# Each column part of the last four down tiles loaded by three transfers of 112, 8 and 8 partitions instead of one of 128

## The chip, the cores and the metric

The kernel runs on one core of one Trainium2 chip. The metric is the device time of one execution in microseconds (us): lower is better. The times given are medians of several executions; the profile shows one execution, with its own time beside it.

## The reference, cut to what matters

One layer of a trunk for 128 context tokens and 128 latent tokens (256 in all), model width 1024, float32. After the token mixers comes a mixture of 64 experts, and its weights are nearly all that the kernel loads: three arrays of 64 x 1024 x 256 float32, 64 MB each.

```python
def expert_block(args):
    tb, gb = args
    a = jax.nn.silu(jnp.einsum('td,edf->tef', tb, w_gate)) * jnp.einsum('td,edf->tef', tb, w_up)
    return jnp.einsum('tef,efd->td', a * gb[..., None], w_down)
...
x = x + g2 * moe_ffn(hn, ...)
```

Every expert's gate and up projection (1024 to 256) and its down projection (256 back to 1024) are applied to the tokens routed to it, the results are summed over the experts per token, and a gated residual gives the outputs `y_prompt` and `y_sample`.

## The kernel before

**Tiles and loops.** The weights of an expert are three tiles of 1 MB (gate, up, down), each 128 partitions x 8 KB. Four experts make a unit; 16 units are computed in sequence, the experts ordered by how many tokens they got. The tiles rotate through a ring of twelve places and five more (`spare`, `gb`, `xn`, a place over `yhi`, `rows_tile`); `PLACE` says which tile goes where. The last unit is a "quad" unit: four experts side by side, 32 token slots each.

**Who loads.** SyncE (SP) issues all expert tiles, in one order, in its own program: `released(g)` waits until TensorE has finished with the tile whose place is to be filled, then `load_tile` (L577) issues one 1 MB transfer on all 128 partitions. Its semaphore `tile_loaded[place]` rises by 16 when it has landed. TensorE waits for that semaphore in `weights_ready` before the matmuls that use the tile.

**The end.** The last four down tiles are treated apart. `lay_out_by_columns` has arranged `w_down` so that a range of output columns is contiguous in each partition. `FINAL` names three column parts in the order in which they are loaded and computed: columns 512 to 1024, 256 to 512 and 0 to 256. For each part `load_columns` (L649) issues one transfer per tile, twelve in all: 128 partitions x 4 KB (512 KB) for the first part, and 128 partitions x 2 KB (256 KB) for the second and the third. The first two parts count on `last_columns[0]` and `last_columns[1]` (four transfers each, so 64), the third on each tile's own `tile_loaded`. SP starts them when the down matmuls of the quad step before have released the places (`y_filled`, by the matmuls of L1365).

**What uses them.** `down_final` on TensorE (matmuls at L1343) waits for part 0, multiplies, waits for part 1, multiplies, then adds parts 0 and 1 into the token sums (`combine_final`: L1323 with the upper halves `yhi`, L1327 with the rests `ylo`), and then waits for part 2. ScalarE makes `yhi` (L1763) and VectorE `ylo` (L2365) of each of the first two parts; VectorE then multiplies the sums with the gate (`scale`, L2437), GpSimd adds the residual (L835), and SP and ScalarE store the outputs (L531). Part 2 goes by a shorter way: VectorE gates it in place (L2383), TensorE spreads it to tokens (L1318), VectorE adds it (L2388).

**Other names in the diff.** `weights_ready(..., again=True)` is for later rounds, which run only if an expert got more tokens than its slots hold; the trace ends after the first round.

Of the kernel before, what the change touches and what calls it, by code (L numbers as in the profile page):

```python
# [44 lines left out]
PAIR, QUAD = 2, 4  # L45
# [3 lines left out]
NSLOT = 4  # L49
NTILE = 3 * NSLOT  # L50
# [11 lines left out]


UNITS = NE // NSLOT
QUAD_UNITS = {12 // 2 * it + 2 + j for it in range(TURNS) for j in range(2)} | {UNITS - 2, UNITS - 1}
FIRST_STEP = [sum(1 if v in QUAD_UNITS else 2 for v in range(u)) for u in range(UNITS)]

# [5 lines left out]
def place_tiles():  # L73

    place, replaces, free = list(FILL), [None] * len(FILL), []
    taken = 0
    while len(place) < UNITS * NTILE:
        if len(place) == ROWS_FREE:
            place.append(OVER_ROWS)
            replaces.append(None)  # L80
        kept = OVER_Y if len(place) < (UNITS - 1) * NTILE else OVER_GB
        while place[taken] == OVER_Y or (kept == OVER_GB and place[taken] in (OVER_GB, OVER_XN)):
            taken += 1
        place.append(place[taken])
        replaces.append(taken)
        taken += 1
    nth = [place[:g + 1].count(p) for g, p in enumerate(place)]
    return place, replaces, nth


PLACE, REPLACES, NTH = place_tiles()


def build(nc, t, o, overflow_at=CAP):

    ctx = ExitStack()
    with ctx:
# [6 lines left out]
        def sem(name):  # L104
            return ctx.enter_context(nc.semaphore(name))
# [264 lines left out]
        tile_loaded = [sem(f"tile_loaded{i}") for i in range(NTILE + 5)]  # L370
        last_columns = [sem(f"last_columns{i}") for i in range(2)]
# [106 lines left out]
        def tile(i):  # L478
            if i >= NTILE:
                return (spare[:, :], gb[:, :, :].rearrange("p s d -> p (s d)"), xn[:, 0:EW], over_yhl[:, :], rows_tile[:, :])[i - NTILE]  # L480
            return ring[:, i * EW:(i + 1) * EW]
# [3 lines left out]
        down_dram = t["w_down"]  # L485

        def down_columns(weights, f, cols_):

            v = weights.rearrange("p (q j n) -> p j q n", j=JF, q=D // FE)[:, f, cols_.start // FE:cols_.stop // FE, :]
            return v[:, 0, :] if v.shape[1] == 1 else v  # L490

        def tile_of(kind, par, part, j):
            return 4 * part + j if kind == QUAD else 6 * par + 2 * part + j

        def unit_of(kind, par, unit):
            return unit + par if kind == QUAD else unit
# [11 lines left out]
        def final_out(i):  # L508

            return bank[FINAL_BANK[i]][:, FINAL[i].start % 512:FINAL[i].start % 512 + FINAL[i].stop - FINAL[i].start]  # L510
# [22 lines left out]
        def weights_of(kind, par, part, j, unit, again):  # L533

            i = tile_of(kind, par, part, j)
            return tile(i if again else PLACE[unit_of(kind, par, unit) * NTILE + i])

        def weights_ready(pe, kind, par, part, j, unit, again):

            i = tile_of(kind, par, part, j)  # L540
            if again:
                pe.wait_ge(tile_loaded[i], unit * 16 + (PLACE.count(i) * 16 + 16))
            else:
                g = unit_of(kind, par, unit) * NTILE + i
                pe.wait_ge(tile_loaded[PLACE[g]], NTH[g] * 16)
# [6 lines left out]
        def _(sp):  # L552
# [21 lines left out]
            def load_tile(g, e):  # L574
                unit, i = divmod(g, NTILE)
                part = i // 4 if unit in QUAD_UNITS else i % 6 // 2
                sp.dma_start(tile(PLACE[g]), (gate_dram, up_dram, down_dram)[part][e]).then_inc(tile_loaded[PLACE[g]], 16)  # L577
# [50 lines left out]
            def after(step, part, more=0):  # L628

                if part == 0:  # L630
                    sp.wait_ge(gate_used, step + 1)
                elif part == 1:
                    sp.wait_ge(e_filled, step + 1)
                else:
                    sp.wait_ge(y_filled, step * 2 + 2 + more)

            def released(g):

                unit, i = divmod(g, NTILE)
                if unit in QUAD_UNITS:  # L640
                    after(FIRST_STEP[unit], i // 4)
                else:
                    after(FIRST_STEP[unit] + i // 6, i % 6 // 2)

            def load_columns(g, e, i):

                w = FINAL[i]
                v = slice(JF * w.start, JF * w.stop)
                ins = sp.dma_start(tile(PLACE[g])[:, v], down_dram[e][:, v])  # L649
                ins.then_inc(last_columns[i] if i < 2 else tile_loaded[PLACE[g]], 16)  # L650

            def refill(unit, experts, first=0, end=NTILE):

                for i in range(first, end):
                    g = unit * NTILE + i
                    if REPLACES[g] is None:
                        sp.wait_ge(sorted_filled, 1)
                        sp.wait_ge(cnt_ready, 1)
                    else:
                        released(REPLACES[g])  # L660
                    load_tile(g, experts[i % 4 if unit in QUAD_UNITS else 2 * (i // 6) + i % 2])

            def experts_of(unit):
                return [expert_at(NSLOT * unit + j) for j in range(NSLOT)]

            refill(1, range(NSLOT, 2 * NSLOT), first=len(FILL) - NTILE)
            sp.wait_ge(order_ready, 1)
            for unit in range(2, UNITS - 1):
                refill(unit, experts_of(unit))
            experts = experts_of(UNITS - 1)  # L670
            refill(UNITS - 1, experts, end=8)
            released(REPLACES[UNITS * NTILE - 1])
            for i in range(N_FINAL):
                for j in range(NSLOT):
                    load_columns(UNITS * NTILE - NSLOT + j, experts[j], i)
# [169 lines left out]
        def _(pe):  # L845
# [222 lines left out]
            for q in range(2):  # L1068
                ins = nc.tensor.transpose(ps[0:ROWS, q * P:q * P + P], gi[:, q, :], ident[:, :])
# [11 lines left out]
            ins = nc.tensor.transpose(ps[:, 4 * ROWS:4 * ROWS + NH], n0r[:, :], ident[0:NH, 0:NH])  # L1081
# [231 lines left out]
            def combine_final(i):  # L1313

                if i == LAST:
                    for s, y in ((1, act_e), (0, sil)):
                        pe.wait_ge(last_gated, 2 - s)
                        mm(last_sum(s), ptone[:, 1, s * P:s * P + P].bitcast(F32), y[:, :],  # L1318
                           start=True, stop=True).then_inc(all_done, 1)
                    return  # L1320
                pe.wait_ge(y_hi, (STEPS - 1) * 2 + (i + 1))
                for s in (1, 0):
                    mm(final_acc(s, i), ptone[:, 1, s * P:s * P + P], final_y(yhi, i), start=False, stop=False,  # L1323
                       skip_group_check=True)
                pe.wait_ge(y_lo, (STEPS - 1) * 2 + (i + 1))
                for s in (1, 0):
                    mm(final_acc(s, i), ptone[:, 1, s * P:s * P + P], final_y(ylo, i), start=False, stop=False,  # L1327
                       skip_group_check=True).then_inc(all_done, 1)

            def down_final(unit):  # L1330

                w = P // QUAD
                pe.wait_ge(a_copied, STEPS)
                pe.wait_ge(g2_kept, 2 * NST)
                for i, cols_ in enumerate(FINAL):
                    if i < 2:
                        pe.wait_ge(last_columns[i], 16 * NSLOT)
                    else:
                        for j in range(QUAD):
                            weights_ready(pe, QUAD, 1, 2, j, unit, False)  # L1340
                    for f in range(JF):
                        for j in range(QUAD):
                            ins = mm(final_out(i)[j * w:(j + 1) * w, :], actT[:, f, j * w:(j + 1) * w],  # L1343
                                     down_columns(weights_of(QUAD, 1, 2, j, unit, False), f, cols_),
                                     start=(f == 0), stop=(f == JF - 1))
                    ins.then_inc(y_filled, 1)
                    if i == 1:
                        combine_final(0)
                        combine_final(1)
                combine_final(2)  # L1350
# [43 lines left out]
            def two_steps(kind, e, n, group, unit, following, gates=gate_s, before=True, starts=False, shared=None, ends=False,  # L1394
# [40 lines left out]
                if ends:  # L1435
                    down_final(unit)
                else:
                    down(kind, 1, n + 1, unit, group, last, again)
# [1064 lines left out]
```

## Time and profile before

| what | value |
|---|---|
| median of 3 runs | 643.16 us (641.85 to 643.47) |
| the profiled execution, its time | 640.87 us |
| its span, first to last instruction | 639.6 us |
| TensorE matmul, busy | 579.2 us (91%) |
| TensorE weight load, busy | 404.3 us (63%) |
| VectorE, busy | 211.8 us (33%) |
| ScalarE, busy | 167.7 us (26%) |
| read from HBM | 250.06 MB, 394 GB/s over the span |

The page of a profile gives the busy time of each engine, the span cut in 40 slices, and the chain of work that ended last. The trace behind it can be asked for a stretch alone: its instructions in order of time, the chain of waits, the share of the DMA engines that was busy, and for a DMA the time from its issue to its landing. "SPq" is an issue of a DMA by SyncE's queue, "ACTq" one by ScalarE's.

### The profile page before, as it was taken

The page shows a single profiled execution, that of the slowest core. Times are in us where ns is not written, and L with a number is a line of the kernel's source. Part 1 is how long each engine was busy: PE and PEld are TensorE (multiplying, and loading weights), DVE is VectorE, ACT ScalarE, POOL GpSimd, SP SyncE. Part 2 cuts the span into 40 slices and gives each one's busy share as a digit, 9 for nine tenths or more (in the row PEclk, how much of TensorE's full clock was granted, in tenths as well). Part 3 has the DMA queues.
Part 4 walks back from the last instruction along what each step waited for, and adds up shares of the span by engine and source line. Part 5 has one row for each costly group of instructions (what it writes and reads, how often), then busy time and mean ns, then how long its engine had stood idle before and what let it go on. Part 6 is the DMA issues. An engine that isn't in the chain of part 4 may idle for free.

```text
span 639.6 us, 11143 instructions
## 1 busy us (share of the span) xinstructions
PE 579.2 (91%) x4568; PEld 404.3 (63%) x4568; DVE 211.8 (33%) x479; ACT 167.7 (26%) x308; POOL 32.8 (5%) x78
## 2 busy tenths in 40 slices
PE   0899999999999999989999999596999999997775
PEld 0488777788867676657575766364567666664343
DVE  1287867787832222011222121020121212121104
ACT  3164727672622121112121212010212121212110
POOL 1340210011100000000000000000000000000002
PEclk9989999999999999999999999798999999999889
DMA  8999699989999999999999999999999999999994
GB/s 341 386 344 388 216 363 381 409 327 397 419 378 379 404 421 419 422 420 420 421 420 421 420 421 419 421 421 421 421 420 420 421 420 421 420 421 419 422 412 159
DMA packets 49126, 252.55 MB, mean 395 GB/s; under 512 B 5912, under 2 KB 9632, under 8 KB 24752
## 3 DMA queue, kind: packets, MB, share of 16 engines
q1 hardware_dynamic: 46272, 245.85, 94.7%
q0 software_dynamic: 1840, 4.21, 2.0%
q10 hardware_dynamic: 960, 1.74, 0.7%
q8 instruction: 37, 0.61, 0.4%
q14 instruction: 17, 0.14, 0.1%
HBM read 250.06 MB, written 1.72 MB: 394 GB/s over the span
## 4 chain that ended last, share of the span: by engine, by line
PE 56%; DMA 20%; SPq 16%; ACT 4%; DVE 2%; issue 2%; POOL 0%; POOLq 0%; DVEq 0%; ACTq 0%
PE bank L1291 17%; SPq L577 14%; PE bank L1365 9%; DMA ring<-in_w_up 8%; DMA ring<-in_w_down 7%; PE bank L1262 5%; PE bank L1308 5%; PE bank L861 3%; DMA ring<-in_w_mod 2%; PE bank L903 2%; PE bank L911 2%; PE bank L907 2%; DMA ccol<-in_c 2%; SPq L649 1%; DMA ring<-in_w_in 1%
## 5 line engine op out<-in xcount | busy, mean ns | idle before, releaser
L1291 PE MATMUL bank<-ring,xe 128*64 128x256 f32 (+1 forms) x1520 | 176.4, 395 | 10.5 <-DMA ring<-in_w_up 9.3
L1291 PEld LDWEIGHTS bank<-ring,xe 128*64 128x64 f32 (+1 forms) x1520 | 110.9, 131 | 49.3 <-issue 23.0
L1365 PE MATMUL bank<-ring,actT 128*64 128x512 f32 (+1 forms) x384 | 83.9, 597 | 3.8 <-DMA ring<-in_w_down 2.2
L2339 DVE TENSOR_TENSOR act_e<-bank,sil 128x256 f32<-128x256 f32 x26 | 11.0, 425 | 192.1 <-ACT sil L1754 192.1
L2353 DVE SCALAR_TENSOR_TENSOR ylo<-bank,gslot,yhi 128x512 fp32r<-128x512 f32 x50 | 37.5, 751 | 78.1 <-ACT yhi L1767 78.1
L1767 ACT ACTIVATE yhi<-bank,gslot 128x512 fp32r<-128x512 f32 x50 | 34.4, 688 | 110.7 <-PE bank L1365 110.7
L1754 ACT ACTIVATE sil<-bank 128x256 f32<-128x256 f32 x26 | 10.0, 385 | 195.1 <-PE bank L1291 195.1
L1262 PE MATMUL bank<-pone,hhi 128*128 128x256 f32 x200 | 50.0, 288 | 0.0
L1262 PE MATMUL bank<-pone,hlo 128*128 128x256 f32 x200 | 48.9, 282 | 0.0
L1365 PEld LDWEIGHTS bank<-ring,actT 128*64 128x64 f32 (+1 forms) x384 | 25.0, 127 | 32.5 <-issue 32.3
L1291 PE MATMUL bank<-rows_tile,xe 128*64 128x256 f32 (+1 forms) x128 | 32.9, 416 | 12.5 <-DMA ring<-in_w_up 6.3
L1749 ACT ACTIVATE xe<-bank 128x512 f32<-128x512 f32 x50 | 29.9, 598 | 48.2 <-PE bank L1262 48.2
L1308 PE MATMUL bank<-yhi,ptone 128*128 128x512 f32 x100 | 42.2, 422 | 0.0
L1308 PE MATMUL bank<-ylo,ptone 128*128 128x512 f32 x100 | 39.5, 395 | 0.0
L1262 PEld LDWEIGHTS bank<-pone,hhi 128*128 128x128 f32 x200 | 38.2, 191 | 0.5
L1262 PEld LDWEIGHTS bank<-pone,hlo 128*128 128x128 f32 x200 | 38.1, 191 | 0.6
L1291 PE MATMUL bank<-xn,xe 128*64 128x256 f32 (+1 forms) x128 | 31.8, 406 | 3.3 <-DMA ring<-in_w_up 3.3
L1291 PEld LDWEIGHTS bank<-rows_tile,xe 128*64 128x64 f32 (+1 forms) x128 | 17.3, 137 | 25.1 <-issue 19.1
L1291 PE MATMUL bank<-spare,xe 128*64 128x256 f32 (+1 forms) x128 | 31.8, 406 | 0.0
L1291 PE MATMUL bank<-gb,xe 128*64 128x256 f32 (+1 forms) x128 | 31.8, 406 | 0.0
L835 POOL TENSOR_TENSOR xn<-xn,xt 128x512 f32<-128x512 f32 (+1 forms) x3 | 3.4, 1165 | 462.9 <-DVE xn L2437 462.9
L1308 PEld LDWEIGHTS bank<-yhi,ptone 128*128 128x128 f32 x100 | 18.7, 187 | 13.1 <-issue 9.8
(388 smaller groups left out, 849.0 us busy)
## 6 DMA issues: line engine op xcount, KB each, us to landing
ring<-in_w_gate SPq DMA_DIRECT2D x49, 1024.0 KB, 25.3
ring<-in_w_down SPq DMA_DIRECT2D x48, 1024.0 KB, 26.3
ring<-in_w_up SPq DMA_DIRECT2D x46, 1024.0 KB, 26.6
ring<-in_w_mod SPq DMA_DIRECT2D x12, 2048.0 KB, 13.6
ring<-in_w_in SPq DMA_DIRECT2D x5, 2048.0 KB, 15.4
gb<-in_w_up SPq DMA_DIRECT2D x5, 1024.0 KB, 25.3
spare<-in_w_gate SPq DMA_DIRECT2D x4, 1024.0 KB, 26.9
ring<-in_w_out SPq DMA_DIRECT2D x2, 2048.0 KB, 18.7
```

The source lines that it names most:

```text
L577: sp.dma_start(tile(PLACE[g]), (gate_dram, up_dram, down_dram)[part][e]).then_inc(tile_loaded[PLACE[g]], 16)
L861: ins = mm(ps[r:r + P // CT, 0:MW], csil[:, CT * a + k, :], w[:, k, MW * c:MW * c + MW], start=(a == 0 and k == 0), stop=(a == 1 and k == ...
L903: mm(ps[s][:, 0:w], xhi[:, k, s * P:s * P + P], proj_upper(c)[:, k, :], start=(k == 0), stop=False)
L907: mm(ps[s][:, 0:w], xlo[:, k, s * P:s * P + P], proj_upper(c)[:, k, :], start=False, stop=False)
L911: ins = mm(ps[s][:, 0:w], xhi[:, k, s * P:s * P + P], proj_rest(c)[:, k, :], start=False, stop=(k == KD - 1))
L1262: ins = mm(ps[:, k * 256:k * 256 + 256], h[:, s, 2 * q + k, :], pone[:, s, :, :].rearrange("p a b -> p (a b)"), start=(i == 0), stop=(i == 3))
L1291: ins = mm(bank[6][j * w:(j + 1) * w, part * FE:(part + 1) * FE], xe[:, k, slots], weights[:, k, :], start=(k == 0), stop=(k == KD - 1))
L1308: ins = mm(acc[s][n][:, :], ptone[:, par, s * P:s * P + P], y[:, n, :], start=(first and y is yhi), stop=False, skip_group_check=True)
L1365: ins = mm(bank[4 + h][j * w:(j + 1) * w, :], actT[:, f, j * w:(j + 1) * w], down_columns(weights_of(kind, par, 2, j, unit, again), f, sli ...
L1749: A(xe[:, 2 * q:2 * q + 2, :], bank[(7, 4, 5, 7)[q]][:, :].rearrange("p (a b) -> p a b", a=2), ACT.Copy).then_inc(x_copied, 1)
L1767: A(yhi[:, n, :], bank[4 + n][:, :], ACT.Copy, scale=gslot[:, par:par + 1]).then_inc(y_hi, 1)
L2353: V.scalar_tensor_tensor(out=ylo[:, n, :], in0=bank[4 + n][:, :], scalar=gslot[:, par:par + 1], in1=yhi[:, n, :].bitcast(F32), op0=ALU.mul ...
```

## The change

A tuple of three partition ranges is added, and each column part of each of the last four down tiles is issued once per range: 36 transfers instead of 12, of the same bytes. The counts that TensorE waits for grow with the number of transfers. Nothing else changes.

```diff
+LAST_ROWS = (slice(0, 112), slice(112, 120), slice(120, 128))
...
@@ weights_ready (later rounds only)
             if again:
-                pe.wait_ge(tile_loaded[i], unit * 16 + (PLACE.count(i) * 16 + 16))
+                more = (len(LAST_ROWS) - 1) * (i in PLACE[UNITS * NTILE - NSLOT:])
+                pe.wait_ge(tile_loaded[i], unit * 16 + ((PLACE.count(i) + more) * 16 + 16))
...
@@ load_columns
                 w = FINAL[i]
                 v = slice(JF * w.start, JF * w.stop)
-                ins = sp.dma_start(tile(PLACE[g])[:, v], down_dram[e][:, v])
-                ins.then_inc(last_columns[i] if i < 2 else tile_loaded[PLACE[g]], 16)
+                for rows_ in LAST_ROWS:
+                    ins = sp.dma_start(tile(PLACE[g])[rows_, v], down_dram[e][rows_, v])
+                    ins.then_inc(last_columns[i] if i < 2 else tile_loaded[PLACE[g]], 16)
...
@@ down_final
                     if i < 2:
-                        pe.wait_ge(last_columns[i], 16 * NSLOT)
+                        pe.wait_ge(last_columns[i], 16 * NSLOT * len(LAST_ROWS))
                     else:
                         for j in range(QUAD):
-                            weights_ready(pe, QUAD, 1, 2, j, unit, False)
+                            at = PLACE[UNITS * NTILE - NSLOT + j]
+                            pe.wait_ge(tile_loaded[at], (PLACE.count(at) - 1 + len(LAST_ROWS)) * 16)
```

## Rows read from the trace of the kernel before

**Rows 1.** The page, throughput of the DMA engines in 40 slices of the span.
```profile
GB/s 341 386 344 388 216 363 381 409 327 397 419 378 379 404 421 419 422 420 420 421 420 421 420 421 419 421 421 421 421 420 420 421 420 421 420 421 419 422 412 159
```

**Rows 2.** Chain of waits, 560 to 640 us: start, duration, what.
```profile
600.48 3.67 PE bank L1365 x32
...
613.15 15.50 DMA ring<-in_w_down
...
628.70 1.11 PE bank L1343 x16
...
630.34 0.38 DVE ylo L2365
...
630.77 0.70 DVE xn L2437
...
631.54 0.94 POOL xn L835
```

**Rows 3.** Busy time of each engine by stretch, and the DMA engines' share.
```profile
622.00:624.00 2.00, 2.00 (x37) 1.24 (x30) 0.00 (x0) 0.03 (x1) 0.00 (x0) 1.00 1.07 404
...
625.00:626.00 1.00, 1.00 (x7) 0.78 (x6) 0.42 (x1) 0.00 (x0) 0.00 (x0) 1.00 0.65 240
...
628.00:629.00 1.00, 0.47 (x12) 0.22 (x12) 0.00 (x0) 0.69 (x1) 0.00 (x0) 1.00 0.50 191
629.00:630.00 1.00, 1.00 (x17) 0.49 (x10) 0.75 (x1) 0.17 (x1) 0.00 (x0) 1.00 0.20 78
```

**Rows 4.** Packets from 628.7 to 631.3 us.
```profile
DMA packets 83, 0.14 MB, mean 55 GB/s; under 512 B 13, under 2 KB 13, under 8 KB 83
```

**Rows 5.** The page, queue that loads instructions: packets, MB, share of 16 engines.
```profile
q8 instruction: 37, 0.61, 0.4%
```

**Rows 6.** L649 from 615.2 us: the ninth transfer, issue, time to landing.
```profile
L649 SPq DMA_DIRECT2D spare<-in_w_down x1: 1921/1921/1921, 615.2 to 615.2; - x1
...
DMA to landing us min/median/max: 14.1/14.1/14.1
```

**Rows 7.** L649 from 618.8 us: the twelfth transfer, issue, time to landing.
```profile
L649 SPq DMA_DIRECT2D ring<-in_w_down x1: 2879/2879/2879, 618.8 to 618.8; - x1
...
DMA to landing us min/median/max: 12.4/12.4/12.4
```

**Rows 8.** Timeline, 627 to 632 us: start, duration, engine, line, operation.
```profile
627.13 0.60 PE L1343 MATMUL bank<-ring,actT 128*32 128x512 f32 x3
...
627.56 0.60 PE L1343 MATMUL bank<-ring,actT 128*32 128x512 f32 x3
628.23 0.69 ACT L1763 ACTIVATE yhi<-bank,gslot 128x512 fp32r<-128x512 f32 x1 [3.88 <-PE bank L1343]
...
629.02 0.75 DVE L2365 SCALAR_TENSOR_TENSOR ylo<-bank,gslot,yhi 128x512 fp32r<-128x512 f32 x1 [1.05 <-ACT yhi L1763]
...
631.37 0.38 PE L1343 MATMUL bank<-spare,actT 128*32 128x256 f32 x1
```

**Rows 9.** Chain of waits, the first five issues of L649.
```profile
604.31 0.33 SPq L649
...
604.82 0.52 SPq L649
...
606.63 1.99 SPq L649
```

**Rows 10.** Timeline of the start: two transfers of 8 partitions, three of 2 MB.
```profile
1.29 0.66 ACTq L1485 DMA_DIRECT2D bnr<-in_norm_w  x1
...
1.98 0.28 ACTq L1486 DMA_DIRECT2D bnr<-in_norm_w  x1
...
2.32 5.91 SPq L566 DMA_DIRECT2D ring<-in_w_mod  x3
```

**Rows 11.** The page, issues of full down tiles: count, KB each, median us to landing.
```profile
ring<-in_w_down SPq DMA_DIRECT2D x48, 1024.0 KB, 26.3
```

**Rows 12.** DMA issues from 560 us: an output store, median us to landing.
```profile
out_y_sample<-xn SPq DMA_DIRECT2D x1, 256.0 KB, 2.0
```

## Prediction

> **What bounds the kernel now.** I read the page's throughput slices first. From the fifteenth slice on they stand at 419 to 422 GB/s nearly without a break until the last two [rows 1]: the kernel is a stream of weights, and its end follows from when the last bytes land. So the question is the last 35 us. The chain of waits there says it plainly: the down matmuls of L1365 release the places at about 604.2, SP issues the twelve column transfers of L649, the eighth of them (part 1 of the last tile), issued at 613.15, takes 15.50 us and lands at 628.65, and TensorE starts part 1 at 628.70. Then come ScalarE's `yhi` (in between), VectorE's `ylo`, VectorE's `scale`, and GpSimd's residual at 631.54, which leads to the last stores [rows 2]. The third view is the stretches: the DMA engines are all busy until 624 (share 1.07, which is full), but only 0.65 from 625, 0.50 from 628 and 0.20 from 629 [rows 3]. The bytes are not short of bandwidth there; about half of the 16 engines have finished by 625 or 626, and the other half is still working. After part 1 has landed only some 70 packets of 2 KB remain (0.14 MB; the other 13 of the 83 are under 512 B), out of 512 that part 2 has [rows 4]. So the late engines set part 1 and part 2, and the early ones idle for up to 5 us.
>
> Why half of them is late can be estimated. The queue that loads instructions took 0.4% of 16 engines' span, in 37 packets [rows 5]: 0.004 x 16 x 639.6 = 41 us of one engine. If it falls on eight engines, it makes each of them 5.1 us late, about what the stretches show. That is an estimate; no row names an engine.
>
> **Part by part: the balance of rows.** A part's transfer has 128 rows, and one row is one packet [rows 4]; over 16 engines that is eight rows each. With 112 rows it is seven each. The two transfers of 8 rows can use at most eight engines each. If both go to the same eight, those carry 9 rows per tile and part and the others 7. If these others are the late ones, they lose one row in eight. The price of a row: the ninth transfer lands at 615.24 + 14.1 = 629.3 [rows 6] and the twelfth at 618.84 + 12.4 = 631.2 [rows 7], so three transfers of 2 KB rows take 1.9 us on the last engine, 0.64 each, 0.08 per row, and 0.16 for a 4 KB row. Until the end of part 1 that is four rows of 4 KB and four of 2 KB, 0.64 + 0.32 = 0.96 us earlier; until the end of part 2 it is 1.28 us. The early engines finish later by as much, at 626 or 627 instead of 625 or 626, and still in time.
>
> **What is late next.** Part 1 would land at 628.65 - 0.96 = 627.69. But TensorE is still in part 0: its last matmuls start at 627.56, 0.43 after those before them, so part 1 can start at about 628.0 [rows 8]. It gains 0.7, not 0.96. Behind it, ScalarE has `yhi` of part 0 until 628.92 and VectorE `ylo` of part 0 until 629.77 [rows 8]; VectorE can start `ylo` of part 1 at about 629.8 instead of 630.34 [rows 2], 0.54 earlier. `scale` then starts at about 630.3 instead of 630.77, and GpSimd follows. The gain that reaches the end is **0.5 us**. Part 2 would land at 631.2 - 1.3 = 629.9, and TensorE comes to it at 630.9 instead of 631.37 [rows 8]: no wait there. The bounds are 0 (another order of the same engines) and 0.96 (all of part 1's gain).
>
> **Part by part: the issues.** SP issues 36 transfers instead of 12. Four pitches before, from 604.31 to 606.63, are 0.58 us each, with durations of 0.33 and 0.52 and a gap of about 0.18 between two [rows 9]. For a transfer of 8 partitions the trace has two, on ScalarE's queue: 0.66 and 0.28 us [rows 10]. So a new pitch lies between 0.28 + 0.18 = 0.46 and 0.66 + 0.18 = 0.84; I take 0.58, since that is the same line and queue in the same state. The last issue then begins at 604.31 + 35 x 0.58 = 624.6, and lands at 626.6 at the earliest, with the 2.0 us of a store of 256 KB [rows 12] as latency. It is needed at 631.3. So the 24 added issues cost nothing, hidden behind the stream; without that cover they would cost 24 x 0.58 = 14 us. Behind them on SP stand only the stores, the first of which waits for GpSimd's work at 631.54 [rows 2]. The second term is whether SP is held. Before, the fifth issue took 1.99 us instead of 0.33 [rows 9], with some ten transfers in flight (a full tile lands 26.3 us after its issue [rows 11], and 1.05 MB at 421 GB/s [rows 1] are 2.5 us). At the start of the kernel SP was held with far fewer but larger ones: three of 2 MB took 5.91 us [rows 10]. So it is room for rows that runs out, not for transfers, and the rows stay the same. A few more entries for completion are added (two per tile and part on eight engines); I price them at nothing, and at 0.5 us at most. TensorE's waits have other counts and the same place.
>
> The 8-row transfers move 32 and 16 KB. The Trainium skill ("DMA: Bandwidth & Descriptors", Rules for kernel authors) says of such sizes that under 64 KB one pays mostly overhead, and to coalesce; its fixed cost of about 2 us, paid 24 times in a row, would make 48 us. That no run of this case pays it in series is told by ten transfers in flight at a time [rows 11].
>
> **Rivals.** *The rows go to the wrong eight.* If the 8-row transfers fall on the late engines, part 1 lands 0.96 later, 629.6, and the whole chain behind it moves: **+0.95 us**, 644.1. Nothing in the rows names the engines, so only the form speaks: a fixed choice of eight either hits the late set or misses it. The same page (Why a DMA increments its semaphore by 16 and not by 1) says that a transfer uses the largest number of engines up to 16 that divides its partitions, the lowest-numbered ones; by that 112 gives 16 engines and 8 gives the first eight, but which half fetches instructions it doesn't say.
>
> *Nothing changes.* The 8-row transfers alternate over all engines, or another wait stands at once behind part 1: **0**, 643.2. The same page's rule for two transfers to disjoint partitions (don't bother, they share the same engines) would give this. Against it: eight rows can't be on 16 engines.
>
> *SP becomes the bound, the case that ends slower.* The place is the last issues of part 2. It decides from a pitch of (631.3 - 2.0 - 604.31) / 35 = 0.71 us on. At 0.84 the last issue begins at 633.7 and lands at 635.7: **+4.4 us**. If instead SP is held by the number of transfers, it has issued ten by 620, when the last full tile is through, and the other 26 need 15 us: the last lands at 637.2, **+5.9**. For it: 0.66 in one row. Against: 0.28 in the other, and the pitch of 0.58 with four times the rows and more.
>
> **How the numbers follow.** The profiled execution has a span of 639.6 and a time of 640.87, 1.3 around the span; the median of the runs is 2.3 above that. I put the difference on the median: 643.16 - 0.5 = **642.7 us**. Chances: the forecast 0.47, the wrong eight 0.18, nothing changes 0.22, SP the bound 0.10, and 0.03 for a gain that I don't see. The range takes in the first three: from the lowest run less the upper bound of the gain, 641.85 - 0.96 = 640.9, to the highest run plus the loss, 643.47 + 0.95 = 644.4. Left out is SP as the bound, and half of the unseen gain. About 0.3% (1.9 us) is what a measurement of this kernel can tell from no change, and the first three cases all lie within it: 0.86. Slower by more is SP's case and a little for two losses at once, 0.11; faster 0.03.
>
> **What the profile after would show.** If the forecast holds: 36 issues of L649, done by about 625; the DMA share from 628 on below 0.50 and higher from 625; TensorE's idle time before part 1, now 628.70 - 628.16 = 0.54 us, near 0; `ylo` of part 1 directly behind that of part 0. If the wrong eight are loaded: that idle time grows to about 1.5 us, the DMA share stays high after 629. If SP is the bound: the last issue of L649 begins after 629, and TensorE waits before part 2. Wrong would be the prediction if the 24 issues are held (2 us each), or if the late engines are not a fixed set.

## The result, and the profile after

The changed kernel takes 650.47 us (median of four runs, 649.19 to 651.68) beside 642.5 us for the kernel before (640.64 to 646.54). The ratio is **1.012, with a 95% interval of 1.0076 to 1.0165**: slower, and outside the range that was forecast (642.7 us, 640.9 to 644.4). Two disturbed runs of it, at 744 and 2044 us, are left out. The profiled execution has a span of 648.5 us and a time of 649.75, against a span of 639.6 and 640.87 before. So 8.9 us have to be found. In the file after the change L649 is now L652, L1343 is L1347, L1291 is L1294 and L1211 is L1214.

The page's throughput slices are read first, as before [rows 1]. This is the page of the kernel after, from its start to its end:

```profile
GB/s 339 385 329 384 225 359 389 410 333 397 419 327 423 406 417 420 418 421 422 421 419 421 420 421 419 420 420 421 421 419 422 419 423 421 420 419 421 408 242 133
```

Before the last three slices only the twelfth and the thirteenth differ by more than 15 GB/s, and their sum hardly does (750 against 757). The second last slice has 242 GB/s instead of 412. A low value could mean that the DMA engines had run out of work. The stretches tell that they had not. First one row of the kernel before, then the kernel after; the last three columns are TensorE's granted clock, the DMA engines' busy share, and GB/s:

```profile
616.00:620.00 4.00, 3.00 (x14) 2.28 (x13) 0.00 (x0) 2.39 (x4) 0.00 (x0) 1.00 1.02 410
```

```profile
612.00:616.00 4.00, 4.00 (x55) 2.33 (x48) 0.00 (x0) 0.00 (x0) 0.00 (x0) 0.84 1.02 370
616.00:620.00 4.00, 3.08 (x15) 2.37 (x13) 0.00 (x0) 2.39 (x4) 0.00 (x0) 1.00 1.04 234
620.00:624.00 4.00, 0.00 (x0) 0.00 (x0) 0.00 (x0) 0.00 (x0) 0.00 (x0) 0.94 1.01 222
624.00:628.00 4.00, 3.16 (x32) 1.77 (x36) 0.00 (x0) 0.00 (x0) 0.00 (x0) 0.50 1.01 264
632.00:634.00 2.00, 2.00 (x16) 1.09 (x18) 0.82 (x3) 0.00 (x0) 0.00 (x0) 1.00 0.89 249
634.00:636.00 2.00, 1.45 (x16) 0.24 (x8) 1.22 (x4) 0.48 (x1) 0.00 (x0) 1.00 0.64 226
```

Two columns have to be read together. The share stays at 1.01 to 1.04, as before, while the throughput is 234 and 222 GB/s where it was 410. **The engines work all the time and move 57% of the bytes**, so a packet occupies its engine nearly twice as long (410 / 234 = 1.75). The fall begins between 612 and 616, while full 128-partition up tiles are still in the queues: they are slowed too.

What this does to TensorE is seen in its timeline: start, duration, line, and in brackets the idle time before and its releaser. First one row of the kernel before, then the kernel after:

```profile
620.25 3.66 PE L1291 MATMUL bank<-ring,xe 128*32 128x256 f32 x64 [1.25 <-DMA ring<-in_w_up]
```

```profile
617.62 1.46 PE L1214 MATMUL bank<-g2row,ident 98*128 98x256 f32 x6
624.84 6.35 PE L1294 MATMUL bank<-ring,xe 128*32 128x256 f32 x64 [5.76 <-DMA ring<-in_w_up]
...
633.53 0.63 PE L1347 MATMUL bank<-ring,actT 128*32 128x512 f32 x3
...
636.48 0.40 PE L1347 MATMUL bank<-spare,actT 128*32 128x256 f32 x1 [1.03 <-DMA ring<-in_w_down]
...
639.47 0.38 PE L1347 MATMUL bank<-spare,actT 128*32 128x256 f32 x1 [0.31 <-DMA ring<-in_w_down]
```

With the rows of before at the same places, TensorE's way to part 0 is 7.3 us longer:
- **The last up tile: 4.6 us.** Its matmuls start at 624.84 instead of 620.25. The bytes agree: before, from 612 to 620.25, the engines moved 4 x 413 + 4 x 410 + 0.25 x 399, about 3390 KB (413 and 399 GB/s are the stretches beside the 410 shown). After, from 612 to 624.84, they moved 4 x 370 + 4 x 234 + 4 x 222 + 0.84 x 264, about 3530 KB. The tile lands after nearly the same bytes, only the bytes come more slowly.
- **TensorE's clock: 2.7 us.** The same 64 matmuls take 6.35 instead of 3.66 us. The granted clock from 624 to 628 is 0.50, the lower of its two levels (1.2 instead of 2.4 GHz), where it was 1.00 before [rows 3]. The engine had been idle for 5.76 us just before. So part 0 starts 4.6 + 2.7 = 7.3 us late, at 633.52 instead of 626.24.

Part 0 is not what ends last, though. Part 1 starts 7.8 us later (636.48 against 628.70 [rows 2]) after a wait of 1.03 us for its transfer, and part 2 starts 8.1 later (639.47 against 631.37 [rows 8]) after a wait of 0.31. The chain of waits of the kernel after, start and duration, runs past TensorE's late matmuls:

```profile
604.35 0.35 SPq L652
...
604.88 0.33 SPq L652
...
605.40 0.28 SPq L652
...
615.16 3.28 SPq L652
...
631.11 8.22 DMA ring<-in_w_down
...
639.47 1.10 PE bank L1347 x16
```

SP starts the column transfers when the places are released, at 604.2 in both kernels, and after that none of its issues waits for TensorE. So **8.1 of the 8.9 us are the late start of part 2, set by its landing**, which the slow packets delay. The up tile and the clock lie beside it: at the higher clock, TensorE would have come to part 1 2.7 us earlier and waited that much longer for the same landing. The two ways are nearly level, and in some of the runs below it is the up tile and the clock that end last.

The other 0.8 us come behind part 2, most of them in one addition of VectorE, before and after; why it took longer is not shown:

```profile
633.42 0.41 DVE L2443 TENSOR_TENSOR xn<-xn,xt 128x256 f32<-128x256 f32 x1
```

```profile
641.39 1.39 DVE L2447 TENSOR_TENSOR xn<-xn,xt 128x256 f32<-128x256 f32 x1
```

The chain also shows SP, which the prediction watched most. Its first issues start 0.52 us apart (604.35, 604.88, 605.40) while nothing holds them: the forecast's 0.58 was about right. From 609 on SP is held by queues that drain slowly, and the last issue comes at 631.11 instead of 624.6. Its transfer still takes 8.22 us to land, where one issued as late in the strided run below takes 2.19: what is late is the queue, not the issue.

### The profile page after: what moved, and what is told of

Read it like the earlier page. It is cut to its first block, busy times and chain, and to the rows that moved or that the text cites. A ratio compares the mean times of both kernels' runs of the same rounds, so it can differ in the third digit from the quotient of the medians.

```text
span 648.5 us, 11215 instructions
## 1 busy us (share of the span) xinstructions
PE 581.8 (90%) x4568; PEld 405.2 (62%) x4568; DVE 212.6 (33%) x479; ACT 167.5 (26%) x308; POOL 32.5 (5%) x78
## 4 chain that ended last, share of the span: by engine, by line
PE 48%; SPq 28%; DMA 17%; issue 3%; ACT 2%; DVE 2%; DVEq 0%; ACTq 0%
SPq L579 23%; PE bank L1294 14%; PE bank L1369 7%; DMA ring<-in_w_down 5%; DMA ring<-in_w_up 4%; PE bank L1265 4%; DMA ring<-in_w_in 4%; SPq L652 4%; PE bank L1311 3%; PE bank L864 3%; DMA ring<-in_w_mod 2%; PE bank L906 2%; PE bank L914 2%; PE bank L910 2%; DMA ccol<-in_c 2%
## 5 line engine op out<-in xcount | busy, mean ns | idle before, releaser
L1294 PE MATMUL bank<-ring,xe 128*64 128x256 f32 (+1 forms) x1520 | 179.1, 404 | 14.7 <-DMA ring<-in_w_up 13.8
L1294 PEld LDWEIGHTS bank<-ring,xe 128*64 128x64 f32 (+1 forms) x1520 | 111.8, 133 | 55.3 <-issue 29.7
L1294 PE MATMUL bank<-rows_tile,xe 128*64 128x256 f32 (+1 forms) x128 | 32.9, 416 | 12.5 <-DMA ring<-in_w_up 6.3
L1294 PE MATMUL bank<-xn,xe 128*64 128x256 f32 (+1 forms) x128 | 31.8, 406 | 3.2 <-DMA ring<-in_w_up 3.2
L1294 PEld LDWEIGHTS bank<-rows_tile,xe 128*64 128x64 f32 (+1 forms) x128 | 17.2, 136 | 25.1 <-issue 19.1
L1294 PE MATMUL bank<-spare,xe 128*64 128x256 f32 (+1 forms) x128 | 31.8, 406 | 0.0
L1294 PE MATMUL bank<-gb,xe 128*64 128x256 f32 (+1 forms) x128 | 31.8, 406 | 0.0
L906 PE MATMUL bank<-w_upper_over,xhi 128*128 128x512 f32 (+1 forms) x96 | 24.4, 403 | 2.9 <-ACT w_upper_over L1579 2.5
```

What stands on the lines that cost most here:

```text
L906: mm(ps[s][:, 0:w], xhi[:, k, s * P:s * P + P], proj_upper(c)[:, k, :], start=(k == 0), stop=False)
L1294: ins = mm(bank[6][j * w:(j + 1) * w, part * FE:(part + 1) * FE], xe[:, k, slots], weights[:, k, :], start=(k == 0), stop=(k == KD - 1))
```

## Experiments

**The narrow transfers left out.** The two transfers of 8 partitions were what the change added, so they came first.

```diff
-LAST_ROWS = (slice(0, 112), slice(112, 120), slice(120, 128))
+LAST_ROWS = (slice(0, 112),)
```

> Twelve column transfers of 112 partitions; the rows 112 to 127 of the last four down tiles are not loaded (left out), so one eighth less is to be moved. Theory U (uneven split: with seven rows per engine the engines no longer keep to partitions of their own and get in each other's way, so each packet takes nearly twice as long): the packets slow down as in the changed kernel, the throughput falls to about 230 GB/s from 614 us on, and the time is 5 to 8 us above before although 0.5 MB less is loaded. Theory N (narrow transfers: the 8-row ones do it): nothing slows, the time is up to 1 us below before. Theory C (number of transfers, 36 for 12): as N.

Measured: 649.95 us, ratio 1.0121 (1.0091 to 1.0152). Stretches:

```profile
616.00:620.00 4.00, 4.00 (x42) 2.75 (x35) 0.00 (x0) 0.65 (x2) 0.00 (x0) 0.92 1.00 210
620.00:624.00 4.00, 1.63 (x8) 1.10 (x6) 0.00 (x0) 1.74 (x3) 0.00 (x0) 0.94 1.02 206
```

One eighth of the last bytes is not loaded at all, with twelve transfers as before, and it is just as slow. The transfers of 8 partitions are not needed for it, nor is the number of transfers. Here the chain of waits does run through the up tile and its matmuls (5.13 us, in part at the lower clock), and TensorE waits for neither part 0 nor part 1:

```profile
594.98 32.16 DMA ring<-in_w_up
...
627.28 5.13 PE bank L1294 x64
```

**Two halves of 64.**

```diff
-LAST_ROWS = (slice(0, 112), slice(112, 120), slice(120, 128))
+LAST_ROWS = (slice(0, 64), slice(64, 128))
```

> Each column part in two transfers of 64 partitions, 24 in all, all of the work done. Theory U: a half of the partitions is written by all 16 engines, so they get in each other's way again, and the time is 5 to 9 us above before, with packets nearly twice as long. Theory N (only transfers of 8 rows are harmful) and theory C (the number of transfers: 12 added instead of 24, so half of the cost at most): 0 for N, at most 4 us for C.

Measured: 649.12 us, ratio 1.0102 (1.0077 to 1.0127).

```profile
616.00:620.00 4.00, 4.00 (x37) 3.02 (x30) 0.00 (x0) 1.21 (x3) 0.00 (x0) 1.00 1.04 248
620.00:624.00 4.00, 0.81 (x4) 0.38 (x2) 0.00 (x0) 1.18 (x2) 0.00 (x0) 1.00 1.01 239
```

An even division does it as well.

**36 transfers of 128 partitions.** The count of the change, but each part's columns are cut into a half and two quarters.

```diff
-LAST_ROWS = (slice(0, 112), slice(112, 120), slice(120, 128))
+LAST_ROWS = (0, 2, 3)
...
-                v = slice(JF * w.start, JF * w.stop)
-                for rows_ in LAST_ROWS:
-                    ins = sp.dma_start(tile(PLACE[g])[rows_, v], down_dram[e][rows_, v])
+                n = JF * (w.stop - w.start) // 4
+                for q in LAST_ROWS:
+                    v = slice(JF * w.start + n * q, JF * w.start + n * (q + (2 if q == 0 else 1)))
+                    ins = sp.dma_start(tile(PLACE[g])[:, v], down_dram[e][:, v])
```

> 36 transfers as in the changed kernel, but each of all 128 partitions, with the columns cut in three (a half and two quarters). Theory U and theory N: packets keep their pace per byte, save for the overhead of smaller ones (1 KB and 512 B rows in part), and the time is within 2 us of before. Theory C: as the changed kernel, 8 us above before.

Measured: 644.95 us, ratio 1.0048 (1.0033 to 1.0063), 3 us.

```profile
616.00:620.00 4.00, 4.00 (x34) 3.09 (x27) 0.00 (x0) 1.33 (x3) 0.00 (x0) 1.00 1.02 394
620.00:624.00 4.00, 2.94 (x48) 1.95 (x50) 0.00 (x0) 1.06 (x2) 0.00 (x0) 1.00 0.98 328
```

The throughput holds where it collapsed in the change. Count and shorter rows together cost a third of the loss, in another way: SP's last issue comes at 632.75 and lands only 2.25 us later, so here the issues end last, and TensorE waits 2.00 us for part 2. The last experiment tells count and rows apart.

**112 and 16.** One narrow transfer less.

```diff
+LAST_ROWS = (slice(0, 112), slice(112, 128))
```

> Each column part in two transfers of 112 and 16 partitions, 24 in all; 16 rows can use all 16 engines, so nothing is moved between engines. Theory U: as the changed kernel, 6 to 9 us above before. Theory N: 0 to 1 us. Theory C: at most 4 us.

Measured: 649.45 us, ratio 1.0111 (1.0092 to 1.0131), with 212 and 219 GB/s in the same two stretches. The same as the change.

**The source moved from HBM to SBUF.** A slow packet may wait for its reading or its writing. Both kernels copy the last down tiles from an SBUF tile instead of loading them (the weights of these tiles are left out), once in one piece of 128 partitions, once in two of 64.

```diff
-                    ins = sp.dma_start(tile(PLACE[g])[rows_, v], down_dram[e][rows_, v])
+                    ins = sp.dma_start(tile(PLACE[g])[rows_, v], ws[rows_, v])
```

> The last four down tiles are not read from HBM but copied, in twelve transfers of 128 partitions, from the shared expert's weights that lie in SBUF, each partition from itself (so the last unit's down weights are wrong: the values are left out). It is the measure for the next run. Both theories: within 2 us of before, since the stream stays full until the end; a little less if reading HBM was what limited.

> The same source in SBUF, but each column part in two transfers of 64 partitions (values of the last down tiles left out as before). Theory U-SBUF (the engines collide on the way into or out of SBUF, since a half of the partitions is reached by a half of the ways): the throughput falls to 220 to 250 GB/s from 615 us on and the time is 5 to 9 us above that of the 128-partition copy. Theory U-HBM (the order in which rows are read from HBM collides): no loss against the 128-partition copy, under 1 us.

Measured: 641.46 us in one piece, ratio 0.9999 (0.998 to 1.0019); 647.85 in halves, ratio 1.0102 (1.0064 to 1.014). First the one piece, then the halves:

```profile
616.00:620.00 4.00, 4.00 (x35) 2.83 (x28) 0.00 (x0) 1.03 (x2) 0.00 (x0) 0.89 1.01 412
```

```profile
616.00:620.00 4.00, 3.29 (x16) 2.55 (x14) 0.00 (x0) 2.39 (x4) 0.00 (x0) 1.00 1.03 240
620.00:624.00 4.00, 0.00 (x0) 0.00 (x0) 0.00 (x0) 0.00 (x0) 0.00 (x0) 0.99 1.00 227
```

With no HBM read in these transfers the loss is the same, so the cause is not how the pieces lie in HBM. It is at SBUF, or in how the engines share out its partitions; these two runs don't tell which, nor reading from writing.

**Two transfers of 64, even and odd partitions.** Count, size of rows, bytes and work are those of the two halves; only which partitions belong to a transfer differs.

```diff
+LAST_ROWS = (slice(0, 128, 2), slice(1, 128, 2))
```

> Each column part in two transfers of 64 partitions, but one takes the even and the other the odd partitions, instead of the lower and the upper half; all of the work done. If what counts is how many ways into SBUF the 64 partitions of one transfer reach (all of them here), the loss is much smaller than with halves: 0 to 3 us above before, packets of 4 KB at 160 to 200 ns. If any split other than that of 128 partitions makes the engines collide, the loss is the same as with halves, 6 to 8 us, packets of 4 KB at 270 ns.

Measured: 641.53 us, ratio 0.9989 (0.9972 to 1.0006).

```profile
616.00:620.00 4.00, 3.84 (x20) 2.96 (x16) 0.00 (x0) 1.92 (x4) 0.00 (x0) 1.00 1.02 412
620.00:624.00 4.00, 2.97 (x56) 2.23 (x60) 0.00 (x0) 0.47 (x1) 0.00 (x0) 1.00 1.04 397
```

All 7 us are gone. **It is the choice of partitions that decides**, not that a transfer has fewer than 128.

**The change in part 2 alone.** Here the up tile and parts 0 and 1 are loaded in front of the new transfers.

```diff
-                for rows_ in LAST_ROWS:
+                for rows_ in (LAST_ROWS if i == 2 else (slice(0, 128),)):
...
-                        pe.wait_ge(last_columns[i], 16 * NSLOT * len(LAST_ROWS))
+                        pe.wait_ge(last_columns[i], 16 * NSLOT)
```

> The split into 112, 8 and 8 only in part 2 (the last 1 MB); parts 0 and 1 in transfers of 128 partitions. Theory U: the tile of the up weights that the last gate and up step waits for lands as before (about 620), TensorE's clock does not fall behind it, and only part 2 is slow: 1 MB at 240 instead of 420 GB/s is 1.9 us more, and the time is 1.5 to 3 us above before. If the loss came from the issues or from a wait, it would be a third of 8 us or more, with SyncE's last issue after 628.

Measured: 643.48 us, ratio 1.0021 (1.0003 to 1.0038), 1.2 us, a little less than the 1.5 to 3 expected.

```profile
616.00:620.00 4.00, 3.63 (x16) 2.87 (x16) 0.00 (x0) 2.12 (x4) 0.00 (x0) 1.00 1.00 408
620.00:624.00 4.00, 2.83 (x53) 2.09 (x57) 0.00 (x0) 0.27 (x1) 0.00 (x0) 1.00 1.05 345
624.00:628.00 4.00, 3.23 (x26) 1.88 (x18) 1.51 (x4) 0.38 (x1) 0.00 (x0) 1.00 0.93 217
```

The fall is there, but later: 217 GB/s at a share of 0.93, where before the same stretch had 248 at 0.66. The up tile's matmuls start at 621.17, the granted clock stays at 1.00, and most of the loss is gone. So the up tile's delay and the fall of the clock come from splitting parts 0 and 1, which are in flight *beside* the last full tiles. Parts 0 and 1 themselves, unsplit here, came late: TensorE waited 1.05 and 1.23 us for them. How much of that is the slow rate isn't told, since SP started them 3.5 us later in this execution.

**A probe: which engines serve 8 partitions?** The kernel before, plus two small loads behind the twelfth transfer, of 8 and of 16 partitions. GpSimd marks the landing of each.

```diff
+            for i, n in enumerate((8, 16)):
+                sp.dma_start(hT[0:n, i, :], t["w_down"][0][0:n, 256 * i:256 * i + 256]).then_inc(wout_loaded[i], 16)
...
+            for i in range(2):
+                pool.wait_ge(wout_loaded[i], 32)
+                pool.memset(hT[0:8, 2 + i, 0:8], 0.0)
```

> The kernel before, with two small loads issued by SyncE behind the last column transfer: one of 8 partitions, one of 16, each of 1 KB rows into memory that is free by then; GpSimd waits for each and then writes a few elements of the same tile, which marks the time. If the 8 engines that a transfer of 8 partitions uses are those that finish early, the first mark stands at 624 to 627, and only the second, which needs all 16 engines, at 631 or later. If they are the late ones, both marks stand at 631 or later. The time is within 1 us of before.

Measured: 641.92 us in a single run. GpSimd's timeline:

```profile
632.10 0.09 POOL L843 MEMSET hT<- 8x8 f32 x1 [462.33 <-DMA hT<-in_w_down]
632.41 0.10 POOL L843 MEMSET hT<- 8x8 f32 x1 [0.21 <-DMA hT<-in_w_down]
```

In the kernel before the early engines were through by 625 or 626 [rows 3], and here the load of 8 partitions, issued at 623.2, lands only at 632.1, with the last of all. So at least one of the engines that serve it is a late one. This speaks for the rival of the wrong eight. It is told by one load from partitions 0 to 7, not from 112 to 127.

**120 partitions.** If the boundary has to lie on a multiple of 8, this one does.

```diff
+LAST_ROWS = (slice(0, 120),)
```

> Twelve transfers of 120 partitions from the first on; the rows 120 to 127 of the last four down tiles are left out. 120 rows are eight for each of 15 engines, in the same blocks of eight partitions, while 112 were seven for each of 16. If the collisions come from blocks that are out of step with groups of four or eight partitions, 120 is nearly free: within 2 us of before. If every contiguous split other than 128 collides, it is 6 to 9 us above before, like 112.

Measured (rows 120 to 127 left out): 648.96 us, ratio 1.0102 (1.0076 to 1.0128), with 228 and 218 GB/s. It is slow as well. Of the contiguous divisions I tried, 112, 64 and 120, all collide; only the full 128 does not.

**The balance by itself.** The kernel before, with part 1 of the last tile cut into 16 transfers of 8 partitions, the partitions of each four apart, in the hope that only the early engines move this piece.

```diff
+                if i == 1 and g == UNITS * NTILE - 1:
+                    for a in range(16):
+                        r = slice(32 * (a // 4) + a % 4, 32 * (a // 4) + a % 4 + 29, 4)
+                        sp.dma_start(tile(PLACE[g])[r, v], down_dram[e][r, v]).then_inc(last_columns[i], 16)
+                    return
...
-                        pe.wait_ge(last_columns[i], 16 * NSLOT)
+                        pe.wait_ge(last_columns[i], 16 * (NSLOT if i == 0 else NSLOT + 15))
```

> The aim of the change without its form: eleven column transfers of 128 partitions, and the eighth (part 1 of the last tile) in 16 transfers of 8 partitions each that lie four apart, so that it is moved by eight engines alone; all of the work done. If the eight are the early ones and the balance of engines is what counts, part 1 lands 0.6 us earlier than before and TensorE's wait before it goes. If the late engines' partitions are limited by their way into SBUF and not by the engine, nothing is gained, since the same bytes still go there: part 1 lands at the same time or up to 1 us later. The time is within 2 us of before in both, so part 1's start behind the end of part 0 is what to read.

Measured: 644.86 us, ratio 1.0044 (1.0024 to 1.0064). The groups of this line, durations in ns as min/median/max, and TensorE at parts 1 and 2:

```profile
L652 SPq DMA_DIRECT2D ring<-in_w_down x16: 650/650/1292, 615.2 to 628.7; - x16
```

```profile
631.21 0.40 PE L1348 MATMUL bank<-spare,actT 128*32 128x256 f32 x1 [0.93 <-DMA ring<-in_w_down]
...
636.09 0.38 PE L1348 MATMUL bank<-spare,actT 128*32 128x256 f32 x1 [2.19 <-DMA ring<-in_w_down]
```

This is **inconclusive on the balance**. An issue of 8 strided partitions occupies SP for 0.65 us, sixteen of them took from 615.2 to 629, and parts 1 and 2 were late for that (waits of 0.93 and 2.19 us). I wanted to measure engines and measured SP.

**Three transfers, dealt out with a stride.** The count of the change, rows of full length, all work done.

```diff
-LAST_ROWS = (slice(0, 112), slice(112, 120), slice(120, 128))
+LAST_ROWS = (slice(0, 128, 2), slice(1, 128, 4), slice(3, 128, 4))
```

> The change's own count of transfers (36, three for each column part), but the rows are dealt out with a stride instead of in blocks: even partitions (64 rows), every fourth from 1 (32), every fourth from 3 (32). All work is done, rows keep 4 and 2 KB. If contiguous blocks of less than 128 partitions are what makes the packets collide: full speed in 616 to 620 us (400 GB/s or more), no long wait for the last up tile, and a time within 1.5 us of before, ratio 0.998 to 1.003. If it is the unequal size of the parts (64, 32, 32 against the two equal halves that ran at full speed), the throughput falls to 210 to 250 GB/s there and the time rises by 6 to 8 us, ratio about 1.01. If 36 issues cost something of their own, as the 36 column transfers left open (they had shorter rows too): 2 to 3 us over before with the throughput of 616 to 620 still at 400; then count is the price, otherwise the short rows were.

Measured: 642.76 us, ratio 1.001 (0.999 to 1.003). Stretches, the groups of SP's issues, and TensorE at part 2:

```profile
616.00:620.00 4.00, 4.00 (x43) 2.60 (x33) 0.00 (x0) 0.55 (x1) 0.00 (x0) 0.86 1.03 419
```

```profile
L652 SPq DMA_DIRECT2D ring<-in_w_down x27: 477/477/975, 610.2 to 631.9; - x27
```

```profile
634.23 0.38 PE L1347 MATMUL bank<-spare,actT 128*32 128x256 f32 x1 [1.11 <-DMA ring<-in_w_down]
```

Full throughput at 36 transfers, with unequal pieces. That leaves the contiguous blocks as the cause. It also settles what the 36 column transfers left open: their 3 us came mostly from the shorter rows, since 36 transfers with full rows cost nothing that can be measured. They are at their limit, though. In this execution SP issued from 608.0 to 631.9, a pitch of 23.9 / 35 = 0.68 us (the 36 column transfers took 25.7 us for the same 35 pitches). The last piece, issued at 631.91, lands 2.19 us later, the chain of waits runs through it, and TensorE waited 1.11 us for part 2: here SP's issues end last. The places had come free later than before (608.0 against 604.31), since the down matmuls ahead, 3.67 us in [rows 2], took 6.27 here; so the wait is not the pitch's alone.

## Why the prediction was wrong

**The step that failed** is the price of a row. "0.08 per row, and 0.16 for a 4 KB row" was taken from transfers of 128 partitions and carried over to transfers of 112 and 8 as if a packet cost the same whichever transfer it belongs to. The rows then only had to be counted per engine. Measured, the packets took nearly twice as long (234 GB/s at a share of 1.04, against 410 at 1.02), those of the full tiles in the queues included. A balance that promised 1 us at the most was paid for with a rate that was 43 to 44% lower from 616 to 624 (234 and 222 GB/s against 410 and 399) and didn't recover.

**No rival had it.** The three were the wrong eight, nothing, and SP. All of them move rows or issues at a fixed price. The range was built from them alone, so it ended at 644.4. The price came from the nearest rows, but no row of before had a partial-partition load inside the full stream. The two 8-partition issues at the start [rows 10] say what SP pays, not what the engines pay. An honest upper bound would have needed a rival of the form "the split transfers move at half the rate": the last four tiles are 4.19 MB, 10.2 us at 410 GB/s and 17.9 us at 234, so +7.7 us (an estimate from the two measured rates), close to the 8.1 by which part 2 was late.

**SP's issues: right in price, wrong in cover.** Unheld, the pitch is 0.52 us (forecast 0.58, bounds 0.46 to 0.84). The bound's upper end is real as well: an issue of 8 strided partitions takes 0.65 us. That SP is held by the room for rows, not for transfers, fits too; but since rows drain at half the rate, SP is held longer and the last issue comes 6.5 us after the forecast. That is a result of the slow packets, not a cause: with strided pieces the last of 36 issues came as late, at 631.91, and the time was 642.76.

**The balance of rows was not tested cleanly.** The probe speaks against its premise, that 8 partitions go to early engines. The direct attempt was limited by SP. What it would be worth at the old packet price stays open.

**The early engines "still in time", "TensorE is still in part 0"**: both fell with the rate. TensorE waited 5.76 us for the last *up* tile, which the prediction did not treat at all, since the change doesn't touch it. And it had no term for the clock: the same matmuls took 2.7 us more at 0.50, after the idle time. In the profiled execution neither set the end, since TensorE still waited 1.03 us for part 1 and 0.31 for part 2; in the run of 112 partitions alone both did.

**The signs listed.** Of "36 issues of L649, done by about 625", the count was right and the end was 631. The last issue after 629 and the wait before part 2 had been named as the signs of SP as the bound, and both came, but the strided run shows the same two without the loss. TensorE's idle time before part 1 grew to 1.03 us and the DMA share after 628 was higher, not lower, which the text had named as the sign of the wrong eight. The sign that told the cause was one it had not listed, GB/s beside the share.

**The page's rule.** The Trainium skill ("DMA: Bandwidth & Descriptors", Rules for kernel authors) advises against two transfers to disjoint partition halves, because they share the same engines and serialize. The prediction read this as a result of 0. The advice was right; the price of nothing that the prediction took from it was not: with two halves the kernel takes 1.0102 times as long, by a fall in the rate of everything in flight.

## What caused it, and what stays open

Shown: the loss needs no HBM read in the split transfers (same source and same destination in SBUF, one piece 412 GB/s, halves 240); it depends on which partitions a transfer covers (halves 248, even and odd 412 GB/s); the narrow transfers and the count aren't needed.

A mechanism was only argued. The Trainium skill ("SBUF — State Buffer", Door 1: The DMA port swizzle) says that DMA bandwidth depends on how many of 16 ports the partitions reach, that four neighbouring partitions share a port, and that partitions 0 to 63 reach eight of the sixteen. Eight of sixteen would be half the rate, an estimate from that page. The traces agree for the halves: 227 to 248 against 412 GB/s, and even or odd partitions, which by that table reach all sixteen, run at 412. They don't bear out the page's sentence (section "Can I just issue two DMAs to hit both halves?") that the only way to hit all 16 ports is one transfer over all 128 partitions: strided pieces of 64 ran as fast as 128. And the table alone does not explain 112 and 120: these reach all sixteen by it, and ran at 206 to 234 GB/s. No row shows which engine takes which partition, so what slows these stays open.

## What to carry to other kernels

In a stream that keeps all DMA engines busy, don't cut a transfer into contiguous blocks of partitions (here it took 40 to 48% off the rate of everything in flight); deal the partitions out with a stride, of which two or three pieces cost nothing measurable. Put the busy share and the GB/s of a stretch side by side: a full share at half the throughput is a slow packet and no lack of work. When costing a new form of transfer at full load, give a rival to "the price of a packet changes, for its neighbours too".

## What the runs showed of the hardware

- Contiguous transfers of 112, 120 or 64 partitions: 206 to 248 GB/s at a busy share of 0.95 to 1.04, where 128 had 410. The transfers of 128 partitions queued beside them are slowed too (370 GB/s already in the stretch from 612, and the last up tile 4.6 us late).
- The same with SBUF as the source: 240 against 412 GB/s.
- The price of an issue on SP depends on the form: unheld, 0.28 to 0.35 us for contiguous blocks of 128, 112 and 8 partitions, 0.47 for contiguous blocks of 64, 0.48 for 32 or 64 strided ones, 0.65 for 8 strided ones.
- After 5.76 us without work TensorE ran 64 matmuls in 6.35 instead of 3.66 us, at a granted clock of 0.50 for most of them. A transfer 4.6 us later put TensorE's next stage off by 7.3; that costs time only where nothing else ends later.
